# Dilated attention: queries and keys of four groups by seven block products in place of eight, and their norms by halves of the tokens

## The reference, cut to what matters

```python
def mixer_a(h, w_qkv, q_gain, k_gain, w_o, cos, sin):        # h: (1, 512, 1024)
    qkv = (h @ w_qkv).reshape(B, S, A_GROUPS, 3, A_HEADS, HEAD_DIM)   # 3 groups, 16 heads of 64
    for g in range(A_GROUPS):                                # dilations 1, 4, 16
        q = partial_rope(rms_norm_2(qkv[:, :, g, 0], q_gain[g]), cos, sin)
        k = partial_rope(rms_norm_2(qkv[:, :, g, 1], k_gain[g]), cos, sin)
        v = qkv[:, :, g, 2]
        num, den, mx = dilated_group(q, k, v, dil, radius)   # windowed softmax, unnormalised
    ...                                                      # weights of the groups by their maxima
    return (num / den[..., None]).reshape(B, S, D_MODEL) @ w_o
```

## Time and profile before

| what | value |
|---|---|
| median of 3 executions | 2879.69 us (2878.11 to 2879.92) |
| the profiled execution | 2885.13 us, its span 2883.2 us |
| TensorE (PE) busy | 2701.0 us, 94% of the span |
| VectorE (DVE) | 1429.2 us, 50% |
| ScalarE (ACT) | 1006.4 us, 35% |
| GpSimd (POOL) | 967.0 us, 34% |
| the stage `dilated` | from about 1395 to 1981 us of the span |

### The profile page before, as it was taken

One profiled execution on the slowest core, in us unless ns is written; L12 is line 12 of the kernel. 1 busy time (PEld: TensorE's weight loads), 2 busy tenths in 40 slices (PEclk: granted clock), 3 DMA queues, 4 the chain that ended last, 5 costly groups with the idle time before them and its releaser, 6 DMA issues. The chain is left out here.

```text
span 2883.2 us, 52215 instructions
## 1 busy us (share of the span) xinstructions
PE 2701.0 (94%) x22635; PEld 2087.6 (72%) x22635; DVE 1429.2 (50%) x2296; ACT 1006.4 (35%) x1632; POOL 967.0 (34%) x408
## 2 busy tenths in 40 slices
PE   7999989888898999888999999998999999999999
PEld 5877877777775433323789978997788878878887
DVE  5435765655543111102543464373676663366766
ACT  4133242343343000001445465554434342243333
POOL 2321431231221000000332323222577654456666
PEclk9999999999999999999999999999999999999999
DMA  7112102113146999999222212122333223323331
GB/s 279 55 34 63 53 17 64 34 32 107 44 167 262 409 427 426 427 427 417 96 75 65 74 61 71 60 69 78 93 97 117 89 88 101 100 91 100 105 98 64
DMA packets 170550, 399.16 MB, mean 138 GB/s; under 512 B 9391, under 2 KB 99476, under 8 KB 144724
## 3 DMA queue, kind: packets, MB, share of 16 engines
q1 hardware_dynamic: 169344, 392.44, 37.0%
q10 hardware_dynamic: 980, 3.40, 0.3%
HBM read 389.45 MB, written 6.29 MB: 137 GB/s over the span
## 5 line engine op out<-in xcount | busy, mean ns | idle before, releaser
L275 POOL TENSOR_TENSOR weight_ring_lo<-weight_ring,weight_hi 128x1024 fp32r<-128x1024 f32 (+2 forms) x230 | 588.4, 2580 | 1380.7 <-ACT weight_hi L250 1326.4
L250 ACT CAST weight_hi<-weight_ring 128x2048 fp32r<-128x2048 f32 (+1 forms) x146 | 221.8, 1522 | 377.1 <-PE late L316 94.2
L275 POOL TENSOR_TENSOR weight_ring_lo<-weight_ring,mlp_more_weight_hi 128x1024 fp32r<-128x1024 f32 x58 | 138.7, 2412 | 174.4 <-ACT mlp_more_weight_hi L250 174.4
L335 PE MATMUL late<-weight_hi,latT_hi 128*128 128x512 f32 x572 | 174.8, 427 | 0.0
L316 PE MATMUL late<-latT_hi,weight_ring_lo 128*128 128x512 f32 x680 | 167.9, 389 | 0.0
L335 PE MATMUL late<-weight_ring_lo,latT_hi 128*128 128x512 f32 x572 | 156.2, 395 | 0.0
L335 PE MATMUL late<-weight_hi,latT_lo 128*128 128x512 f32 x572 | 156.0, 395 | 0.0
L3656 DVE TENSOR_TENSOR x<-x,late 128x512 f32<-128x512 f32 x224 | 143.2, 679 | 18.8 <-PE late L3561 18.8
L316 PEld LDWEIGHTS late<-latT_hi,weight_ring_lo 128*128 128x128 f32 x680 | 127.6, 188 | 26.5
L335 PEld LDWEIGHTS late<-weight_hi,latT_hi 128*128 128x128 f32 x572 | 131.3, 273 | 13.7 <-issue 6.0
L3575 ACT ACTIVATE mlp_hid<-late 128x512 f32<-128x512 f32 x64 | 34.8, 595 | 302.2 <-PE late L316 302.2
(11 more groups left out here) (748 smaller groups left out, 6119.8 us busy)
## 6 DMA issues: line engine op xcount, KB each, us to landing
weight_ring<-in_mlp_w SPq DMA_DIRECT2D x64, 1024.0 KB, 5.2
weight_ring<-in_w_gate SPq DMA_DIRECT2D x36, 1024.0 KB, 19.8
weight_ring<-in_a_wqkv SPq DMA_DIRECT2D x36, 1024.0 KB, 5.1
weight_ring<-in_w_down SPq DMA_DIRECT2D x28, 1024.0 KB, 18.7
weight_ring<-in_w_mod SPq DMA_DIRECT2D x24, 1024.0 KB, 5.5
weight_ring<-in_w_up SPq DMA_DIRECT2D x21, 1024.0 KB, 15.1
weight_hi_spare<-in_w_down SPq DMA_DIRECT2D x15, 1024.0 KB, 21.4
x<-in_w_up SPq DMA_DIRECT2D x12, 1024.0 KB, 24.9
```

The costliest lines, as they stand in the source:

```text
L250: self.nc.scalar.copy(self.hi_view(item)[:, :, 0:w], item.raw()[:, :, 0:w]).then_inc(self.hi_ready, 1)
L275: last = self.nc.gpsimd.tensor_tensor(item.lo()[:, k, 0:w], item.raw()[:, k, 0:w], self.hi_view(item)[:, k, 0:w].bitcast(F32), ALU.subtract)
L335: last = nc.tensor.matmul(dst, left(a, HK * r + k), right(b, k), start=(r + a + b + k == 0), stop=(r == 1 and a == 1 and k == HK - 1))
```

## The change

In groups 1, 2, 4 and 5 (`PAIR_GROUPS`) q and k are computed together as a 2x2 block product. The rows of the left operand are the two halves of the token tiles, its columns the two halves of the 1024 summed rows. The right operand has the blocks b11 and b12 (rows 0 to 511 of the weights of q and of k) and b21 and b22 (rows 512 to 1023). Seven items of 2 slots take the place of eight quarter results of 2 slots, so such a group has 14 + 8 = 22 slots, and `N_SLOT` falls from 144 to 136. The seven items are, in order, b11, b21, t2, t1, b12', b22', t4, where `form_seven` has made t1 = b12 - b11, b12' = b22 - b12, t2 = b22 - t1, t4 = b21 - t2 on VectorE. Items with t are in `a_num` and `a_own`.

Products four to seven on the left side need four sums of token blocks, made once in group 0 (`form_sum`, 10 operations of 128x1024, four casts on ScalarE, four `lower_sum`). Results of single products are copied or added (`copy_block`, `add_block`) into q and k. Squares are now taken from SBUF, and norms are done for two token tiles at a time, in four blocks per group. The first half of the output is kept in DRAM for a while (`o_kept`), `a_near` is halved, several buffers lie elsewhere. The last `turn_in` begins 3 slots before the end of the slots instead of 4.

```diff
+    def add_four(self, w, c1, c2):
+        place = lambda i, c, end: self.place(((w[rows(i), c:c + WIDE], 0),), (HK, WIDE, WIDE), SLOTS, end)
+        b11, b12 = place(0, c1, t), place(0, c2, t + 4)
+        b21, b22 = place(1, c1, t + 1), place(1, c2, t + 5)
...
+        add(raw(b11), low(b11), panel=b11, settled=t1)
+        add(raw(b21), low(b21), panel=b21, settled=t4)
+        add(*own(1), formed=t2, settled=t4)
+        add(*own(0), formed=t1, settled=t2)
+        add(raw(b12), low(b12), formed=t3, settled=t3)
+        add(raw(b22), low(b22), panel=b22, settled=t2)
+        add(*own(2), formed=t4, settled=t4)
...
-LAST_TURN = N_SLOT - 4
+PAIR_GROUPS = (1, 2, 4, 5)
+LAST_TURN = N_SLOT - 3
...
             for m in range(N_TIME):
+                for n in range(N_GROUP):
+                    if 2 <= m - TURNS[n] < 4:
+                        turn_in(n, m - TURNS[n])
                 if m < N_SLOT:
                     project(m)
...
                 for n in range(N_GROUP):
-                    t = m - (PER_GROUP * (n + 1) if n + 1 < N_GROUP else LAST_TURN)
-                    if 0 <= t < 4:
-                        turn_in(n, t)
+                    if 0 <= m - TURNS[n] < 2:
+                        turn_in(n, m - TURNS[n])
...
+                for n in PAIR_GROUPS:
+                    for unit, jj in {6: ((0, 0),), 7: ((0, 1),), 11: ((1, 0),), 12: ((1, 1),), 13: ((2, 0), (2, 1)), 15: ((3, 0), (3, 1))}.get(m - START[n], ()):
+                        square_block(n, unit, jj)
+                    for i, jj in {3: ((0, 0), (0, 1)), 5: ((2, 0),), 6: ((2, 1),), 7: ((3, 0),), 8: ((3, 1),), 13: ((6, 0),), 14: ((6, 1),)}.get(m - START[n], ()):
+                        copy_block(n, i, jj)
+                    if m - START[n] in ROOT_BLOCK:
+                        root_block(n, ROOT_BLOCK.index(m - START[n]))
+                if 0 < m <= N_SLOT:
+                    item = A_SLOTS[m - 1][4]
+                    if m == N_SLOT or A_SLOTS[m][4] != item:
+                        act.wait_ge(st.used, p0 + item + 1)
+                        st.round_until(act, p0 + item + 3)
...
+                    if m == START[n] - FORM_AHEAD:
+                        if n != PAIR_GROUPS[0]:
+                            dve.wait_ge(st.used, p0 + FIRST_ITEM[PAIR_GROUPS[pair_at(n) - 1]] + 7)
+                        st.form_seven(dve, pairs[pair_at(n)])
...
+ROOT_BLOCK = (8, 13, 14, 16)
+NORM_BLOCK = (9, 14, 15, 17)
+FORM_AHEAD = 2
-SPREAD_SLOTS = [(3 * PER_GROUP + s, 3 * PER_GROUP + s) for s in (15, 15, 16, 16, 17, 17, 19, 19, 21, 21, 22, 22)]
+SPREAD_SLOTS = [(START[3] + s, START[3] + s) for s in (13, 13, 14, 14, 15, 15, 16, 16, 17, 17, 18, 18)]
```

More of the change, by code:

```diff
@@ L196, in add_seven @@
         add(*own(3 * turn + 2), formed=t4, settled=t4)
+        return group
+    def add_four(self, w, c1, c2):
+        t = len(self.items)
+        rows = lambda i: slice(i * D // 2, (i + 1) * D // 2)
+        place = lambda i, c, end: self.place(((w[rows(i), c:c + WIDE], 0),), (HK, WIDE, WIDE), SLOTS, end)
+        b11, b12 = place(0, c1, t), place(0, c2, t + 4)
+        b21, b22 = place(1, c1, t + 1), place(1, c2, t + 5)
+        raw = lambda p: lambda: self.view(self.slots[self.slot[p]], p)
+        low = lambda p: lambda: self.view(self.lo[:, self.slot[p]], p)
+        own = lambda i: (lambda: self.pair_own[i], lambda: self.pair_own_lo[i])
+        group = Buffers()
+        group.pair, group.first, group.n = (b11, b12, b21, b22), t, self.n_formed
+        group.b, group.t = [[raw(b11), raw(b12)], [raw(b21), raw(b22)]], [own(i)[0] for i in range(3)]
+        t1, t3, t2, t4 = range(group.n + 1, group.n + 5)
+        self.n_formed = t4
+        add = lambda *parts, **kinds: self.add_item(True, (HK, WIDE, WIDE), *parts, **kinds)
+        add(raw(b11), low(b11), panel=b11, settled=t1)
[5 more added lines that the diff above has]
+        add(*own(2), formed=t4, settled=t4)
         return group
@@ L2870, with dilated_slots @@
 N_GROUP = 6
-PER_GROUP = 6 * NT
-N_SLOT = N_GROUP * PER_GROUP
-LAST_TURN = N_SLOT - 4
+PAIR_GROUPS = (1, 2, 4, 5)
+PAIR_SLOTS = 14
+V_SLOTS = 2 * NT
+def dilated_slots():
+    slots = []
+    item = 0
+    for n in range(N_GROUP):
+        if n in PAIR_GROUPS:
+            slots += [("block", n, i, jj, item + i) for i in range(7) for jj in range(2)]
+            item += 7
+            parts = (2,)
+        else:
+            parts = (0, 1, 2)
+        for part in parts:
+            for r in range(2):
+                slots += [(part, n, r, j, item) for j in range(NT)]
+                item += 1
+    return slots
+A_SLOTS = dilated_slots()
+START = [next(m for m, slot in enumerate(A_SLOTS) if slot[1] == n) for n in range(N_GROUP)] + [len(A_SLOTS)]
+FIRST_ITEM = [A_SLOTS[START[n]][4] for n in range(N_GROUP)] + [A_SLOTS[-1][4] + 1]
+N_SLOT = len(A_SLOTS)
+LAST_TURN = N_SLOT - 3
+TURNS = START[1:N_GROUP] + [LAST_TURN]
+NORMED = [0, 4, 12, 20, 24, 32, 40]
 LAST_STARTS = [LAST_TURN + t for t in (1, 2, 4, 6)]
@@ L2994, in project @@
+                left, right = lambda a, i: f.yT[a][:, i, tokens], lambda b, i: w[b][:, i, :]
+                if m == 0:
+                    last = dense_behind(nc, flat(acc[j][:]), left, right, lambda k: ahead.ready(pe, k), HK)
+                else:
+                    if m == NT:
+                        ahead.ready(pe, KD - 1)
+                    last = dense_half(nc, flat(acc[j][:]), left, right, r)
                 if j + 1 == NT:
@@ L2997, in project, with block_product @@
                     last.then_inc(filled, 1)
+            def block_product(n, i, jj):
+                block, chain, _, _ = SEVEN[i]
+                dst = flat(acc[2 * chain + jj][:])
+                if i < 2:
+                    pe.wait_ge(emptied, 12 * (n - 1) + 8 + 2 * i + jj + 1)
+                elif i in (3, 6):
+                    pe.wait_ge(added, 4 + 6 * pair_at(n) + {3: 0, 6: 2}[i] + jj + 1)
+                else:
+                    pe.wait_ge(emptied, 12 * n + {2: 0, 4: 2, 5: 4}[i] + jj + 1)
+                if n == PAIR_GROUPS[0] and i == 2 and jj == 0:
+                    pe.wait_ge(o_rounded, 4)
+                    pe.wait_ge(o_lowered, 4)
+                if block < 3:
+                    half, k0 = ((0, 0), (0, HK), (1, HK))[block]
+                    left = lambda a, k: f.yT[a][:, k0 + k, slice(2 * half + jj, None, NT)]
+                else:
+                    left = lambda a, k: (sum_hi, sum_lo)[a][:, block - 3, k, jj * P:(jj + 1) * P]
+                for a, b in ((0, 0), (0, 1), (1, 0)):
+                    for k in range(HK):
+                        last = nc.tensor.matmul(dst, left(a, k), w[b][:, k, :], start=(i in FRESH and a + b + k == 0), stop=(a == 1 and k == HK - 1),
+                                                skip_group_check=i not in FRESH)
+                last.then_inc(st.used if jj else filled, 1)
             def turn_in(n, hp):
@@ L3200, in _ @@
                         exps(u, 1)
-                for i in range(2 * N_GROUP):
+                for i in NEAR_NORMS:
                     if m == norm_slots(i)[1]:
```

377 lines of the change are left out of this document (254 added, 123 removed).

## The result

The change made the kernel slower: 2928.3 us, median of four runs (2926.0 to 2931.1), against 2879.1 (2878.1 to 2879.9) before; ratio 1.0171, 95% interval 1.0154 to 1.0189. The forecast was 2907, with a range up to 2932.

A forecast was written before the change was run, and what follows sets the result against it. TensorE's queue was taken to set the pace in `dilated`. Added waits and slower clock of 54.1 us, less a gain of 27.1, put +27.0 on 2879.7: 2907 us; own range 2888 to 2926, whole range 2873 to 2932.

The forecast's parts named there:

- The sign and the cause: Whole kernel: slower, since every block item has two slots, not four, and TensorE waits; +27.0 us, chance of slower 0.79.
- a): Starts of groups 1, 2, 4 and 5: TensorE waits for the first item, b11, together 20.0 us.
- e): End of group 5: half norms among the sums make the last transposes wait for VectorE; 8.9 us, bounds 3 and 13.
- f): TensorE behind three long waits (groups 1 and 4, end): slower clock, about 1 us each, 3.0; bounds 0 and 8.
- rival 3: Slots 4 to 13 of far groups: ScalarE becomes the bound, four pairs per group lag; +32 us, 2939, chance 0.16.
- b): Pair groups: second item, b21, rounded behind the first `write_q`; wait 3.1 us, four times, 12.6; bounds 9 and 13.
- c): Pair groups: TensorE waits for the fourth item, t1, 1.5 us, four times, 6.0; bounds 0 and 10.
- d): Slot 8: sixth item, b22', rounded behind copies and a root; 0.9 us, four times, 3.6; upper bound 11.
- I cost them at nothing, covered by group 0's products: Group 0: sums of token blocks, their casts and lower parts cost nothing; 17 us if the cover were gone.
- the sign of a missed chain: TensorE waiting for banks (`a_emptied`, the adding operations) would mean the prediction had missed a chain; no size given.
- The gain: Four groups lose two slots each, 22.6 us, and products on sums run at near pace, 3.2; 27.1 with group 3's wait.

The follow-up runs named there:

- e9: Changed kernel with 25 filler identity products on TensorE ahead of the wait for b11 in groups 1 and 4; 2920.8 us, ratio 1.0153 to the kernel before.
- e1: Changed kernel with ScalarE casting the second item, b21, first in the slot where a pair group starts; 2917.9 us, ratio 1.0127 to the kernel before.
- e8: Changed kernel with ScalarE casting the item two ahead first in every block-product slot where a new item begins; 2898.0 us, ratio 1.0065 to the kernel before.
- e2: Changed kernel with t1 formed four slots before a pair group instead of two; 2916.6 us, ratio 1.0128 to the kernel before.

## Why the prediction was right, and where not

**The sign and the cause** held: a block item has two slots to be made, and TensorE waits for items. The idle time was forecast well, the sum of a) to e) being 51.1 us and the idle time +54.3, but partly by luck of its parts.

**f), the clock, is the step that failed:** 3.0 us in the sum, with 8 as its bound, against 22.9. It was mis-sized twice: only waits above 3 us were counted (three of them), where waits of 2.1 us did it too; and each was priced at about 1 us by its first four matmuls. e9 shows 2.1 us directly behind each of the two longest waits, since the slow stretch lasted for the whole product. This alone is 20 us, nearly all of the distance from 2907 to 2928. The measured 2928.3 lies above 2926, the upper end that the forecast had for itself, and inside the whole range only because that leaves room for rival 3, whose mechanism did not come: that much is luck.

**a)** 20.0 forecast, 12.7 measured. Groups 1 and 4: 6.24 and 6.41 against 8.8 and 6.4; the form took the order and time forecast (11.05 us to b11, for 11.9). Groups 2 and 5: none, against 2.4 each; there b11 came at 1570.30 and its product began at 1570.52. Group 1's 6.24 is low because group 0 had already stood for 5.28. **b)** 12.6 against 8.6 (2.22, 2.10, 2.19, 2.10); e1 shows the cause as given. **c)** 6.0 against 4.1 (1.27, 0.77, 1.28, 0.78). **d)** 3.6 against 6.1 (1.48 to 1.57), since norm and pass blocked each other besides the table load. **e)** 8.9 against 9.8 in the waits of the spreads; the mechanism was another: the last transposes did not wait for the norm, the spreads of the weights waited before them.

**"I cost them at nothing, covered by group 0's products"** is the other step that failed. The token sums took 2.0 us an operation instead of 1.2, and group 0 got 6.2 us of waits (5.28 for v's item, and 0.87 just before it for a bank that ScalarE empties). Also unforeseen are 5.4 us in which TensorE's products with v wait for VectorE to copy a result out of its bank (`keep`, L3404 and L3408), and 2.4 for the bank that v of group 2 leaves at the start of group 3 (the sign of a missed chain that the prediction named); e8, where the items are in time, has 1.3 of the former. That makes 12.7 + 8.6 + 4.1 + 6.1 + 9.8 = 41.3 for a) to e), where 51.1 had been forecast, and 6.2 + 5.4 + 2.4 = 14.0 that no term had: 55.3 in all. So the agreement of the idle time is luck in good part. The 1.0 us down to 54.3 is what is left when the two waits that went in group 3 (1.31 and 0.82) are set against small ones that grew.

**The gain** is nearly confirmed: four matmuls on the strided tokens start 0.94 us after the four before, on the sums 0.92, so a slot takes 2.82 and 2.76 us, not 2.72. Of the 3.2 us some 1.9 are there, and the clock's share is between 21.6 and 22.9. Rival 3, ScalarE as the bound, came closer in time (2939) than in mechanism, which e8 rules out.

## What to carry over

When an algorithm saves products by making more operands, count for each operand the time between its earliest possible start and its use, on every engine that handles it, and put what feeds the next product first in each engine's slot: one such edit was worth 30 us here. Price a wait of TensorE at its length plus a slow clock behind it: 2.1 us of it behind each wait for b11 here, and in some runs as much behind waits of 2 us. And when a wait is removed, look first whether the next thing behind it is late as well, as here in group 0 and at the end of group 5.

## What the runs showed of the hardware

- Many short waits came with a slower clock: beside 54 us of added idle time, in waits of 0.3 to 6.4 us, the granted clock was 0.96 over the stage and some 22 us went to slower matmuls, 40% on top. Filler products in two of the waits kept the clock at 1.00 behind them (e9, 1467.70 to 1470.80).
- A float32 sum of two 128x1024 tiles on VectorE, one of them read at every fourth element, took 1.98 us; operations on tiles in one piece took 1.22 and 1.23.
- Four 128x128 operations of VectorE took 5.13 us beside one pass of GpSimd, and 0.89 us without; in e2 four of 128x256 took 5.82 in place of 1.42.
- Multiplying by the identity in float32 took 0.22 us a product of 128x128 on a continuously busy TensorE (two records each in the trace).
